# A two-layer hybrid trunk: the first norm taken per token, the first weights requested ahead, the memory normalised between the first products

## The reference

```python
for layer in range(2):
    proj = rms_norm(x, norm_mix_g) @ w_in + b_in      # 1024 -> 8712 columns
    # conv branch, pooling branch, mLSTM branch, sigmoid gates, output product
    x = x + mixer(proj) @ w_out
    x = x + cross_attention(rms_norm(x, norm_xattn_g), rms_norm(mem, mem_norm_g))
    x = x + (swiglu if layer == 0 else top-2-of-8 experts)(rms_norm(x, norm_ffn_g))
out = rms_norm(x, final_norm_g)

def rms_norm(x, g):  return x * rsqrt(mean(x*x, -1) + EPS) * g
```

## Time and profile before

| | |
|---|---|
| median of 3 runs | 2185.11 us (2183.43 to 2185.27) |
| the profiled execution's own time | 2184.56 us |
| its span in the profile | 2182.8 us |
| PE busy | 2072.6 us, 95% of the span |
| DVE busy | 1647.6 us, 75% |
| ACT busy | 1294.3 us, 59% |
| mean granted clock of TensorE | 0.973 |

### The profile page before, as it was taken

One profiled execution on the slowest core, in us unless ns is written; L12 is line 12 of the kernel. 1 busy time (PEld: TensorE's weight loads), 2 busy tenths in 40 slices (PEclk: granted clock), 3 DMA queues, 4 the chain that ended last, 5 costly groups with the idle time before them and its releaser, 6 DMA issues.

```text
span 2182.8 us, 33584 instructions
## 1 busy us (share of the span) xinstructions
PE 2072.6 (95%) x12944; PEld 1882.2 (86%) x12944; DVE 1647.6 (75%) x1717; ACT 1294.3 (59%) x1121; POOL 13.1 (1%) x71
## 2 busy tenths in 40 slices
PE   6998898989998998899989999999999999999996
PEld 5998898979998998899977888888888888888885
DVE  5888765654445988766557888898988888898886
ACT  4555454434434556354436777777777777777774
POOL 0000000000000000000000000000000000000000
PEclk8999999999999999999988999999999999999998
DMA  5544454435554544454427999999999999999993
GB/s 180 176 145 144 130 172 152 155 113 177 191 176 141 172 136 155 136 174 135 157 96 271 383 329 373 340 364 375 326 378 324 380 327 376 343 362 371 329 375 114
DMA packets 309483, 526.71 MB, mean 241 GB/s; under 512 B 13542, under 2 KB 156550, under 8 KB 309382
## 3 DMA queue, kind: packets, MB, share of 16 engines
q1 hardware_dynamic: 309382, 525.29, 68.8%
HBM read 524.21 MB, written 1.05 MB: 241 GB/s over the span
## 4 chain that ended last, share of the span: by engine, by line
PE 81%; DVE 10%; issue 4%; ACT 4%; DMA 0%; DVEq 0%; ACTq 0%; POOL 0%; SPq 0%
PE ps L1454 25%; PE ps L1456 25%; PE ps L1455 25%; DVE w_lo L971 2%; DVE c L1037 2%; ACT w_hi L648 2%; PE ps L1765 1%; PE ps L1501 1%; ACT w_hi L655 1%; PE ps L1839 1%; PE ps L1568 1%; PE ps L1588 1%; DVE cacc L1021 1%; PE ps L1827 0%; PE ps L1828 0%
## 5 line engine op out<-in xcount | busy, mean ns | idle before, releaser
L971 DVE TENSOR_TENSOR w_lo<-raw,w_hi 128x2048 fp32r<-128x2048 f32 x330 | 752.7, 2281 | 376.4 <-ACT w_hi L648 312.5
L1454 PE MATMUL ps<-w_hi,a_hi 128*128 128x512 f32 (+1 forms) x1472 | 566.1, 385 | 0.5 <-DVE h L1324 0.4
L1456 PE MATMUL ps<-w_hi,a_lo 128*128 128x512 f32 (+1 forms) x1472 | 560.5, 381 | 0.0
L1455 PE MATMUL ps<-w_lo,a_hi 128*128 128x512 f32 (+1 forms) x1472 | 559.7, 380 | 0.0
L648 ACT ACTIVATE w_hi<-raw 128x2048 fp32r<-128x2048 f32 x159 | 301.5, 1897 | 313.9 <-PE ps L1456 305.9
L1454 PE MATMUL ps<-a_hi,w_hi 128*128 128x256 f32 x1520 | 443.1, 292 | 28.7 <-DVE a_lo L971 20.9
L1455 PE MATMUL ps<-a_lo,w_hi 128*128 128x256 f32 x1520 | 437.6, 288 | 0.0
L1456 PE MATMUL ps<-a_hi,w_lo 128*128 128x256 f32 x1520 | 437.5, 288 | 0.0
L655 ACT ACTIVATE w_hi<-raw 128x2048 fp32r<-128x2048 f32 x171 | 328.1, 1919 | 123.4 <-PE ps L1456 123.4
L1454 PEld LDWEIGHTS ps<-a_hi,w_hi 128*128 128x128 f32 x1520 | 299.8, 197 | 31.3 <-issue 22.9
L1456 PEld LDWEIGHTS ps<-w_hi,a_lo 128*128 128x128 f32 x1472 | 276.5, 188 | 53.6
(11 more groups left out here) (268 smaller groups left out, 2192.0 us busy)
## 6 DMA issues: line engine op xcount, KB each, us to landing
raw<-in_moe_w SPq DMA_DIRECT2D x171, 1024.0 KB, 5.9
raw<-in_w_in SPq DMA_DIRECT2D x68, 1024.0 KB, 5.2
mem_t<-in_moe_w SPq DMA_DIRECT2D x56, 1024.0 KB, 5.2
area<-in_moe_w SPq DMA_DIRECT2D x56, 1024.0 KB, 5.6
xf<-in_moe_w SPq DMA_DIRECT2D x56, 1024.0 KB, 5.2
raw<-in_ffn_w SPq DMA_DIRECT2D x33, 1024.0 KB, 5.3
raw<-in_w_mlstm_out SPq DMA_DIRECT2D x8, 1024.0 KB, 4.9
raw<-in_w_out SPq DMA_DIRECT2D x8, 1024.0 KB, 4.9
```

The lines of the kernel that those rows point to most:

```text
L971: return dve.tensor_tensor(dst, whole, as_f32(hi), ALU.subtract)
L1454: pe.matmul(dst, wh, xh, start=start, stop=False, skip_group_check=True)
L1455: pe.matmul(dst, wh, xl, start=False, stop=False, skip_group_check=True)
L1456: return pe.matmul(dst, wl, xh, start=False, stop=stop, skip_group_check=True)
```

## The change

The inputs x and mem are read with tokens on partitions. x comes in two transfers of 128 tokens; ACT squares each and sums along the free axis (`accum_out`), so the statistic is a column 128x2. DVE scales x per token in this layout, PE turns the scaled x into `ps0` to `ps3`, and ACT and DVE take `a_hi` and `a_lo` from there, multiplying by the gain (a transfer and a transpose of its own). The unscaled x is turned too, into `ps4` to `ps7`, for `h`. SP asks for chunks 0 to 2 right behind x and the gain; the 20 parameter transfers follow, then mem, then chunk 3. The memory's statistics, scaling, transposes and copies are placed behind `post` of chunks 0, 1 and 3 (`MEM_STEPS`). The parameters are turned and copied after PE's chunk 0.

```diff
+MEM_STEPS = (0, 1, 3)
...
+        x_tok, mem_tok, xn_tok = (t[:, :, :].rearrange("p (t k) n -> p t (k n)", t=TT) for t in (q_t, k_t, xf))
+        junk = (flat2(cacc), flat2(c31))
+        g_rows, g_first = wdk[0:KB, 0, 0:P], rstd[:, 0, 0:KB]
...
+            for t in range(TT):
+                sp.dma_start(x_tok[:, t, :], w["x"][0, t * P:(t + 1) * P, :]).then_inc(x_in[t], 16)
+            sp.dma_start(g_rows, w["norm_mix_g"][0].rearrange("(r p) -> r p", p=P)).then_inc(g_in, 16)
...
+            for c in range(RAW):
+                load(0, c, chunk_source(0, c))
             sp.wait_ge(const_done, CONSTS)
             params(0)
+            sp.dma_start(mem_tok, w["mem"][0].rearrange("(t p) d -> p t d", p=P)).then_inc(mem_in, 16)
             for layer in range(DEPTH):
-                for c in range(N_MIX):
+                for c in range(0 if layer else RAW, N_MIX):
                     load(layer, c, chunk_source(layer, c))
...
+            def first_norm():
+                for t in range(TT):
+                    act.wait_ge(x_in[t], 16)
+                    act.activation(junk[t], x_tok[:, t, :], ACT.Square, accum_out=x_stat[0][:, t:t + 1]).then_inc(x_ss, 1)
+                act.wait_ge(x_ss, TT)
+                act.activation(x_stat[1], x_stat[0], ACT.Sqrt, bias=eps[:, 0:1], scale=1.0 / D).then_inc(x_std, 1)
+                split(0, 0)
+                act.wait_ge(g_c, 1)
+                for k in range(KB):
+                    if k % 2 == 0:
+                        act.wait_ge(x_t, k // 2 + 1)
+                    ins = act.activation(a_hi[:, k, :], ps[k // 2][:, (k % 2) * T:(k % 2 + 1) * T], ACT.Copy, scale=g_first[:, k:k + 1])
...
+                for c in range(1, SPL):
+                    split(0, c)
+            def mem_std():
+                act.wait_ge(mem_in, 16)
+                for t in range(TT):
+                    act.activation(junk[t], mem_tok[:, t, :], ACT.Square, accum_out=m_stat[0][:, t:t + 1]).then_inc(x_ss, 1)
+                act.wait_ge(x_ss, 2 * TT)
+                act.activation(m_stat[1], m_stat[0], ACT.Sqrt, bias=eps[:, 0:1], scale=1.0 / D).then_inc(m_std, 1)
+            def mem_scale():
+                act.wait_ge(m_rst, 1)
+                for t in range(TT):
+                    act.activation(mem_tok[:, t, :], mem_tok[:, t, :], ACT.Copy, scale=m_stat[2][:, t:t + 1]).then_inc(m_scaled, 1)
+            def mem_copy():
+                for i in range(4):
+                    act.wait_ge(mem_tr, i + 1)
+                    act.activation(flat(mem_t[:, 2 * i:2 * i + 2, :]), ps[4 + i][:, :], ACT.Copy).then_inc(mem_c, 1)
...
+                act.wait_ge(par_c.sem, par_c.at(layer, 1))
+                for c in range(SPL, N_MIX + SPL):
...
+                    if layer == 0 and c - SPL in MEM_STEPS:
+                        (mem_std, mem_scale, None, mem_copy)[c - SPL]()
...
             def input_forget(layer):
+                pe.wait_ge(mem_c, 4)
...
                 for c in range(N_MIX):
                     chunk(layer, c)
+                    if layer == 0 and c == 0:
+                        pe.wait_ge(h_ff.sem, 4)
+                        params(0, 7)
+                    if layer == 0 and c == MEM_STEPS[-1]:
+                        pe.wait_ge(m_scaled, TT)
+                        pe.wait_ge(par_c.sem, 1)
+                        turn_pairs(mem_tok, 4, mem_tr)
...
+            turn_pairs(x_tok, 4, h_t)
+            pe.wait_ge(x_scaled, TT)
+            turn_pairs(xn_tok, 0, x_t)
```

More of the change, by code:

```diff
@@ L266, in trunk @@
         take = iter(range(0, 1144, 8))
+        x_tok, mem_tok, xn_tok = (t[:, :, :].rearrange("p (t k) n -> p t (k n)", t=TT) for t in (q_t, k_t, xf))
+        junk = (flat2(cacc), flat2(c31))
+        g_rows, g_first = wdk[0:KB, 0, 0:P], rstd[:, 0, 0:KB]
+        x_stat, m_stat = ([small[:, f + 2 * i:f + 2 * i + 2] for i in range(3)] for f in (48, 54))
         def table(n):
@@ L289, in trunk @@
         ifb_in = sig("if_bias_landed", 32)
-        x_in = [sem(f"x_landed{i}") for i in range(2)]
+        x_in = [sem(f"x_landed{i}") for i in range(TT)]
+        mem_in, g_in = sem("mem_landed"), sem("first_gain_landed")
         hi_done = sig("hi_done", N_MIX, N_FF, before=RAW)
@@ L849, in mixer @@
-                norm_hi(layer, 0, a_hi)
-                if layer:
+                    first_norm()
+                else:
+                    for j in range(4):
+                        act.wait_ge(h_ff.sem, h_ff.at(layer, j - 3))
+                        square(layer, 0, j)
+                    std(layer, 0)
+                    norm_hi(layer, 0, a_hi)
                     split(layer, SPL - 1)
@@ L885, in dense @@
                         split(layer + 1, c - N_FF)
+            act.sem_inc(hi_done.sem, RAW)
             act.wait_ge(const_done, CONSTS)
[L889 to L896, removed]
             for layer in range(DEPTH):
@@ L1251, in mixer @@
                 lo(wif_lo[:, :, :], wif[:, :, :], wif_hi[:, :, :]).then_inc(wif_split.sem, 1)
-                for c in range(SPL if layer else 1, N_MIX + SPL):
+                for c in range(SPL, N_MIX + SPL):
                     if c < N_MIX:
                         split(layer, c, chunk_len(c))
-                    if c >= SPL:
-                        post(layer, c - SPL)
+                    post(layer, c - SPL)
+                    if layer == 0 and c - SPL == MEM_STEPS[0]:
+                        dve.wait_ge(m_std, 1)
+                        dve.reciprocal(m_stat[2], m_stat[1]).then_inc(m_rst, 1)
                     if N_MIX <= c < N_MIX + SPL - 1:
@@ L1283, in dense @@
                     dve.tensor_tensor(s, s, ps[4 + i][:, :], ALU.add).then_inc(h_ff.sem, 1)
[L1285 to L1298, removed]
             dve.sem_inc(lo_done.sem, RAW)
@@ L1699, in _ @@
             pe.wait_ge(const_done, CONSTS)
[L1700 to L1716, removed]
             pe.sem_inc(pe_chunk.sem, SPL)
             pe.sem_inc(e_pe.sem, SPL)
+            pe.sem_inc(summed.sem, 4)
+            pe.wait_ge(g_in, 16)
+            pe.transpose(ps[7][:, 0:KB], g_rows, ident[0:KB, 0:KB]).then_inc(g_t, 1)
+            for t in range(TT):
+                pe.wait_ge(x_in[t], 16)
+            pe.wait_ge(g_c, 1)
+            turn_pairs(x_tok, 4, h_t)
+            pe.wait_ge(x_scaled, TT)
+            turn_pairs(xn_tok, 0, x_t)
             for layer in range(DEPTH):
```

91 lines of the change are left out of this document (62 added, 29 removed).

## The result

| | before | changed |
|---|---|---|
| median of 4 runs | 2184.27 us (2183.27 to 2185.27) | 2162.71 us (2158.91 to 2165.78) |
| profiled execution, its own time | 2184.56 us | 2162.14 us |
| its span | 2182.8 us | 2160.3 us |
| mean granted clock | 0.973 | 0.978 |

The changed kernel takes 0.9898 of the time of before, 95% interval 0.9886 to 0.991, so it is 21.6 us faster; 20.8 were forecast (2164.3). Its runs lie further apart than those of before, 6.9 us against 2.0.

What follows compares the result with a forecast made beforehand. PE was taken as the bound, with its idle time at the start worth shortening: 2184.56 - 23.0 (chunk 1 earlier) + 2.4 (memory's transposes) = 2164.0, given as 2164.3 us for the median; range 2161.3 to 2168.5.

Steps and rivals of the forecast that it cites:

- The bound: Whole kernel: PE busy 95% of the span; in the first 38.00 us busy only 16.25, so the start counts.
- First product, 15.7: Start, PE: first product of weights at 15.7 us instead of 38.05.
- rival (c): DVE's scaling of x at the lower bound: step to 22.6 falls 0.9, giving 2163.1; chance 0.65 together with the forecast.
- Chunk 1, 22.6: PE starts chunk 1 at 22.6 instead of 45.63, DVE's low part last, chunk 0 mostly at full clock; 23.0 earlier.
- Given back, 2.4: Between chunks 3 and 4: PE's 16 transposes of the memory, 16 x 0.15, unhidden, cost 2.4 us.
- The cover of 2.4 us: Ahead of the memory's transposes: scaled memory ready at 37.5, PE through with chunk 3 at 39.9.
- (a): Start: the wait for parameters replaces that for weights; rows at 25 give 2167.3, at 28 give 2170; chance 0.12.
- (e): Before chunk 4: PE waits for late scaled memory; mem landing at 55 gives 2187; chance 0.03 with the like.
- ACT's table loads: Ahead of the root on ACT: two loads of 1.28 without drain; with the skill's drain, start 2.8 later, near 2167.
- The rest of the program all shifted alike: Behind the start: the program waits on its own engines' steps, all shifted alike.
- The sum: Whole kernel: 2184.56 - 23.0 + 2.4 = 2164.0 us, given as 2164.3.
- The 0.55 that the forecast added for the median: Whole time: the median of the runs taken to lie 0.55 above the profiled execution.

Runs made afterwards that it cites:

- e2: Kernel before with only chunks 0 to 2 asked for right behind x and mem, ahead of the parameters, norms unchanged; 2177.6 us, 0.9962 of before.
- e3: Changed kernel with chunks 0 to 2 asked for behind the parameters again; 2169.67 us, 0.9932 of before.
- e4: Changed kernel with mem asked for behind x and its treatment in front, transposes ahead of chunk 0; 2167.12 us, 0.9919 of before.
- e7: Changed kernel with DVE's scaling of x in a two-input form, second input bypassed; 2163.04 us, 0.9898 of before.
- e5: Changed kernel without the memory's squares, root, scaling, transposes and copies, transfer kept; 2157.97 us, 0.9877 of before.
- e8: Changed kernel with mem asked for behind chunk 3 and the root's table loaded on ACT at the very start; 2161.0 us, 0.9891 of before.
- e6: Changed kernel with mem asked for behind chunk 3 instead of ahead of it; 2158.21 us, 0.989 of before.
- e1: Changed kernel run again with no edit; 2161.31 us, 0.989 of before.

## Why the prediction was right

- **The bound.** That the start's gap on PE is worth its full length held: 21.74 us at the gate columns, 21.6 in the medians. e2, e3 and e4 split it, each part with what it does to the rate of chunk 0. From before to e2 (the loads) 6.60; with the norm by tokens and the memory behind but no loads ahead (e3) 11.94; with the norm and the loads but the memory in front (e4) 15.13; all three 21.74. Put last, the loads are worth 9.80, the memory's place 6.61, and the form of the norms, of x and of the memory alike, with the parameters' transposes put behind chunk 0 (e2 to e4), 8.53. One thing is to be set right on the kernel before: DVE's addition to `lo_done` stands behind the memory's eight products, but SP's first load was released at 19.72, just after the long reciprocal (17.79 to 19.54), while the products ran on to 22.35. So the load waited for the reciprocal and not for the products.
- **First product, 15.7.** 14.91. ACT's sum came out to the tenth (root done at 9.85 against 9.8), partly by luck: the first half of x was there 0.4 later than forecast (4.76 against 4.4), and the two squares took 2.2 and not 2.5. The scalings were mis-sized: 0.71 each (1.42 for the two), where I took 1.22 from the two-input row. The Trainium skill (VectorE: DVE Perf Modes, Mode 2x_2P) gives such a one-input fp32 operation two results per cycle, an estimated 0.7. The trace agrees with the page, and e7 shows both sizes side by side in this place (2.48 against 1.42 for two). I should have given the page's branch more weight; it was rival (c).
- **Chunk 1, 22.6.** 21.29. DVE's low part was ready at 21.1 against 22.4: 1.0 is the scaling, 0.3 the eight low parts of the activations (3.22 us, where 3.5 was taken). That DVE alone would be last did not hold: PE followed from chunk 0 and the parameters' transposes without a gap and was the last, by 0.2. That chunk 0 would run mostly at the full clock held. From its first product to chunk 1's it took 6.25 to 6.83 us in the six traces in which PE had stood at most 2.54 us ahead of it (both of the changed kernel, e5 to e8), and 7.10 to 7.62 in the four in which it had stood 4.11 to 10.69 (before, e2, e3, e4). Where in the first range a run falls is luck.
- **Given back, 2.4.** 1.96 for the transposes, 0.15 to 0.82 of waiting: 2.1 to 2.8. The size is right, but by luck: the transposes were taken 0.44 too long, and the wait was taken as nothing. The cover of 2.4 us that the prediction gave was used up from both sides. PE was through with chunk 3 at 38.8 and not at 39.9, and the scaled memory was there at 38.89 and not at 37.5, since chunk 3 landed at 27.2 instead of 25. Two issues held SP for 5.5 us, and the last parameter transfer was asked for at 16.04 instead of 12.23, 3.8 later, where I had allowed 1 to 2; and mem stood in the queue ahead of chunk 3. e6 shows that the order of these two transfers decides which is late. Rivals (a) and (e) named the two halves of this, neither at its place: the late transfer was the chunk behind mem, by 2.2 us.
- **ACT's table loads.** The row of before said that nothing stands between a load and the next activation; 8.26 + 1.28 = 9.54 and the root's start at 9.56 say so again. The drain of the Trainium skill's page (ScalarE: Activation LUTs, What ACT_TABLE_LOAD costs) would have cost an estimated 2.8 us (twice 1.38) and is not there; the measurement decides.
- **The rest of the program all shifted alike.** Not in each execution. From the gate columns to the router's first product (below) the changed kernel's first trace was 3.1 us shorter than that of before (1027.1 against 1030.2), and from there to the end 2.4 longer (1049.1 against 1046.7). That the whole span agrees with the start to 0.8 owes to these two cancelling.
- **The sum.** 23.0 won and 2.4 given back were forecast; 24.1 won and 2.1 given back were measured (chunk 4's first product 62.65 before, 40.67 after: 21.98), and 0.24 went between there and the gate columns. The net error, 20.6 against 21.74, is 1.3 at chunk 1, of which the scaling makes 1.0, less 0.25 for the 45.63 read off too late, plus 0.3 at the memory, less the 0.24: 1.1 in all. In the medians it is 0.8 (20.8 against 21.6, or 23.0 in e1). The 0.55 that the forecast added for the median did not come back: the median of four runs of before lies 0.3 below the profiled execution, and the measured 2162.71 is 1.6 below the 2164.3.

## What to carry to other kernels

At a kernel's start read which of three chains (input, statistic, first weights) ends last, and shorten that; then do the sum again, for each repair makes the next one late (here the weights, then the norm, then the weights again in e8). Work that is needed much later belongs in the idle time of engines behind the first products, but its transfer goes behind the ones that the pipeline needs next (e6: 0.6 and 1.2 us at the gate columns), and its cover has to be worked out with the queue as full as it will be then. A place early in the program tells 0.5 us where the whole time can't tell 3, if the rate of the first chunk is read beside it.

## What the runs showed of the hardware

**The granted clock at the start is not what the profile says.** In the changed kernel it reads 1.00 from 0 to 100 us. But 16 transposes took 3.65 at 6.34 and 3.67 at 11.55, and the same 16 took 1.97 at 10.11 in e8 and 1.96 behind chunk 3; the second and third product of chunk 0 stood 0.21 apart, those from 15.65 on 0.12. These are the distances that chunk 0 of before shows in its stretch at 0.51 and behind it at 1.00. So PE began at the low level (1.2 GHz) and rose to the high one (2.4 GHz) at a place that differs: before 11.5 in e5, at 15.6 in the changed kernel's trace. PE's timeline of e5:

```profile
11.49 1.97 PE L1705 MATMUL ps<-ident,xf 128*128 128x128 f32 x16 [1.55 <-DVE xf L1304]
```

The trace of before carries the same sign: its first 16 took 3.65 as well, and the window of 5 to 17 us shows 1.00:

```profile
5.00:17.00 12.00, 10.11 (x49) 9.09 (x50) 5.34 (x8) 4.78 (x6) 0.00 (x0) 1.00 0.52 152
```


**Where the runs part.** From the gate columns to layer 1's last stage ahead of the experts (the router's first product) PE's instructions are the same in all these kernels, and yet the traces took 1030.2 us (before), 1027.1 (changed), 1032.2 (e1), 1029.7 (e2), 1025.8 (e3), 1028.6 (e4), 1030.0 (e5), 1027.4 (e6), 1030.2 (e7) and 1030.6 (e8). Of the 5.1 by which e1 is slower than the first trace of the changed kernel, 2.6 had come up by 1075.67, and 2.5 more come behind one pause late in layer 1. PE's timeline there, the changed kernel first, then e1:

```profile
1075.67 1.97 PE L1654 MATMUL ps<-z_sig,vx 128*128 128x256 f32 x8 [3.95 <-DVE xf L1162]
```

```profile
1078.90 3.75 PE L1654 MATMUL ps<-z_sig,vx 128*128 128x256 f32 x8 [3.95 <-DVE xf L1162]
```

And the 20 us from there on, in the same order:

```profile
1075.67:1095.67 20.00, 20.00 (x157) 19.69 (x158) 8.63 (x8) 6.14 (x6) 0.00 (x0) 1.00 0.50 176
```

```profile
1078.90:1098.90 20.00, 20.00 (x140) 19.28 (x141) 6.48 (x7) 6.12 (x6) 0.00 (x0) 0.87 0.37 127
```

The pause is 3.95 us in both, and the granted clock behind it is 1.00 in one and 0.87 in the other, with 157 and 140 products in 20 us. Behind the same pause on PE the clock fell in one execution and not in the other, and the next products took as much longer. The runs bear this out as a whole. Of the eight executions of the changed kernel (its own four and e1's), the three with a mean granted clock of 0.975 or 0.976 took 2163.28 to 2165.78 us, the five with 0.977 or 0.978 took 2158.91 to 2162.14. All eighteen of before lie at 0.972 or 0.973, within 3 us. So the changed kernel's scatter (6.9 us against 2.0) goes with the clock. Why moving the program by 20 us makes the clock's falls differ more from run to run is not shown.
